# Four rewritten stages and an early half product in a two-block fp32 kernel

## The chip, the cores and the metric

One Trainium2 core of one chip. The time is the device time of one execution in microseconds (us), the median of a few runs; all data are fp32. Engines are TensorE (PE), VectorE (DVE), ScalarE (ACT), GpSimd (POOL) and SyncE (SP), which only starts transfers here.

## The reference

A sequence of 256 tokens of width 1024 goes through a first block of two hybrid attention layers and a second block. Cut to what the change touches:

```python
# first block, each of 2 layers
shift, scale, gate = split(c @ w_ada + b_ada)
h = split_cols((x * (1 + scale) + shift) @ w_in)          # three attention mixers on h
x = layer_norm(ALPHA * x + (1 + gate) * ((mix * silu(h["gate"])) @ w_out), ln_g, ln_b)
# second block
a_in = rms_norm(h_lat) * (1 + sc1) + sh1                  # and the same for a context
o = gdn_two_dirs(...)                                     # 4 chunks of 64 tokens, one after the other
y_a = u * (einsum(ws, rms_norm(v)) + bs)                  # chunk mixer, columns 0:512
y_b = rms_norm(o) * gdn_norm_g * silu(z)                  # from the recurrence, columns 512:1024
h_lat = h_lat + gt1 * (concat(y_a, y_b) @ w_out)
f_in = rms_norm(h_lat, norm2_g) * (1 + sc2) + sh2
aff = softmax(f_in @ w_router + b_router)                 # 16 experts
gate, idx = top_k(aff.T, 32)                              # each expert takes 32 tokens
ye = (silu(xe @ w_gate) * (xe @ w_up)) @ w_down * gate    # xe = f_in[idx]
h_lat = h_lat + gt2 * scatter_add(idx, ye)
return rms_norm(h_lat, final_norm_g)
```

## The kernel before, in words

Each engine has its own written-out program; semaphores order them. `tick`, `fill` and `drain` count events, `wait_ge(*at(event))` waits for one, `free(b)` waits until PSUM bank `b` (eight of 128x512) has been read. Tokens lie in two tiles `t` of 128.

**Weights.** All weights come as units of 2 MB in a fixed order (`unit_order`) that SP starts one by one, in order, each when its slot is free again (L495 to L502). There are 4 slots in `ring`; the experts (16, with 6 units each) use three more, which lie over `QKT`, `Vt_to_O` and `zuv_to_Kt`: the first is filled after the last `QS_mm`, the other two after `mix2` of tile 1. The first 7 expert units are thus in place before the experts begin; the eighth waits for the first expert product (`gu_mm` of expert 0).

**A layer's end.** `pe_y` multiplies the mixed rows by `w_out` in parts; `v_ln` gates, adds, takes the statistics (`bn_stats`, `bn_aggr`), waits for ACT's root (Ln, then Exp with scale -0.5) and normalizes, tile 0 then tile 1. Then the next layer begins: `pe_xT` transposes tile 0, `v_uT` and `a_uT` write its modulated rows, `pe_in` multiplies. DVE reaches `v_uT` of tile 0 only after `v_ln` of tile 1.

**The second block.** `pe_streams` begins after `a_ctx_T`; `a_lat_rs` and `v_lat_rows` normalize the rows; `pe_recur` steps through four chunks (products WS, QS, KV, AV). After it come the chunk mixer's product (`ws_mm`), `v_mix2` (norm of `O` and both halves of `wide`), and in `pe_mix2`, for each tile, two halves of four transposes and two column groups of eight products (128x512). `v_mix2` multiplies by `grow` (gt1), adds to `resid`; `a_route` takes the squares' sum and the root; `v_n2` scales rows; `pe_route` transposes them, `v_route` and `a_route` apply norm2_g, scale and shift into `fT`, and 16 router products (128x16) follow. Then softmax, four rounds of `max` and `match_replace`, a mask `selT`, its transpose, three products for positions, `Pone`, and the gather products `xe_mm` (16 of 128x512). POOL copies a column into `selg` so that `pe_grow(1)` can spread gt2 over rows; this and `v_grow(1)` stand ahead of the router.

**Experts and end.** Per expert: four `gu` units, activation, transposes, two `down` units, both halves of `ye` copied out of PSUM (ACT the first, DVE the second), and four products that accumulate in banks 0 to 3 (`moe_mm`). `v_final` multiplies by `grow`, adds `resid`, waits for ACT's squares and root, scales by it and by `fin_row`; SP sends out one tile at a time.

A fp32 product of 128x512 is two TensorE instructions in the trace, a transpose of 128x128 one.

## Time and profile before

| | us |
|---|---|
| median of 3 runs (lowest, highest) | 1344.79 (1342.96, 1347.21) |
| the profiled execution, device time | 1344.98 |
| its span on the core | 1343.2 |
| between the two | 1.8 |
| busy: PE, DVE, ACT, POOL | 1082.7, 429.4, 265.3, 70.0 |

The span is what the profiler sees of the core's engines; the device time has 1.8 us more. Busy shares say little here, since the kernel runs through stages with different limits; the rows below are read stage by stage.

### The profile page before, as it was taken

How to read it: one execution, taken by the hardware profiler on the slowest of the kernel's cores; microseconds unless marked ns; L12 is line 12 of the kernel's file. 1: busy time of each engine (PE TensorE's matmuls, PEld its weight loads, DVE VectorE, ACT ScalarE, POOL GpSimd, SP SyncE). 2: the span in 40 equal slices, each digit the busy share in tenths (PEclk: the TensorE clock that was granted, in tenths of full speed). 3: DMA queues.
4: the chain of work that ended last, by engine and by line, in shares of the span. 5: the costliest groups of instructions: out<-in, count | busy, mean ns of one | idle time of the engine just before them, and what ended most of it. 6: DMA issues, size and time to landing. Idle time of an engine off the chain costs nothing.

```text
span 1343.2 us, 17768 instructions
## 1 busy us (share of the span) xinstructions
PE 1082.7 (81%) x7516; PEld 585.2 (44%) x7516; DVE 429.4 (32%) x1023; ACT 265.3 (20%) x604; POOL 70.0 (5%) x81
## 2 busy tenths in 40 slices
PE   2899999889999999999988868687766666666663
PEld 0344774434576458975678844422221111121111
DVE  0135746323765445343256662400000000000003
ACT  0102134111213435442121343100000000000003
POOL 1001000000100000002204400000000000000000
PEclk9899989989989999899988889697798888889887
DMA  9773238523346961122110035079999999999993
GB/s 375 293 281 108 94 135 340 175 113 126 125 157 258 427 230 73 63 88 102 65 64 3 2 119 210 16 310 428 430 431 430 429 429 429 430 428 431 429 430 132
DMA packets 24270, 323.66 MB, mean 241 GB/s; under 512 B 2704, under 2 KB 2704, under 8 KB 4864
## 3 DMA queue, kind: packets, MB, share of 16 engines
q1 hardware_dynamic: 22160, 314.18, 57.1%
q0 software_dynamic: 2032, 8.35, 1.9%
q8 instruction: 60, 0.98, 0.3%
q14 instruction: 18, 0.15, 0.0%
HBM read 321.47 MB, written 1.05 MB: 240 GB/s over the span
## 4 chain that ended last, share of the span: by engine, by line
PE 54%; DMA 29%; DVE 9%; issue 4%; ACT 3%; POOL 0%; SPq 0%; DVEq 0%; ACTq 0%; POOLq 0%
PE banks L611 45%; DMA ring<-in_stream 18%; DMA Vt_to_O<-in_stream 7%; PE banks L622 2%; DMA zuv_to_Kt<-in_stream 2%; DMA QKT<-in_stream 2%; PE banks L2005 1%; PE banks L836 1%; PE banks L822 1%; DVE Vt_to_O L2263 1%; PE banks L857 1%; PE banks L819 1%; DVE probs L1169 1%; PE banks L723 1%; DMA grow<-in_rows 0%
## 5 line engine op out<-in xcount | busy, mean ns | idle before, releaser
L611 PE MATMUL banks<-ring,uT 128*128 128x512 f32 (+1 forms) x512 | 227.7, 600 | 13.7 <-DVE uT L1028 11.1
L611 PEld LDWEIGHTS banks<-ring,uT 128*128 128x128 f32 x512 | 97.3, 194 | 129.0 <-issue 123.3
L611 PE MATMUL banks<-ring,scr 128*32 128x512 f32 (+1 forms) x656 | 114.8, 695 | 48.0 <-DMA ring<-in_stream 46.0
L611 PE MATMUL banks<-ring,UWK 128*32 128x512 f32 (+1 forms) x368 | 85.9, 718 | 17.8 <-DMA ring<-in_stream 12.1
L2444 DVE SCALAR_TENSOR_TENSOR UWK<-UWK,banks 128x256 f32<-128x256 f32 x16 | 6.7, 421 | 292.5 <-ACT UWK L2697 292.5
L611 PE MATMUL banks<-scr 64*64 64x64 f32 (+2 forms) x2048 | 82.4, 234 | 6.5 <-DVE scr L2311 5.2
L611 PEld LDWEIGHTS banks<-ring,scr 128*32 128x32 f32 (+1 forms) x656 | 30.4, 127 | 125.3 <-DMA ring<-in_stream 70.2
L611 PEld LDWEIGHTS banks<-scr 64*64 64x64 f32 (+1 forms) x2048 | 79.2, 144 | 12.3 <-issue 5.6
L611 PE MATMUL banks<-UWK,ring 128*128 128x256 f32 x320 | 72.6, 386 | 2.1 <-DVE QKT L2087 1.7
L622 PE MATMUL banks<-ring,KC 128*32 128x512 f32 x384 | 50.7, 655 | 26.9 <-DMA ring<-in_stream 26.9
L2005 PE MATMUL banks<-UWK 128*128 128x512 f32 x128 | 58.7, 601 | 16.4 <-DVE UWK L2450 16.4
L611 PEld LDWEIGHTS banks<-UWK,ring 128*128 128x128 f32 x320 | 61.4, 193 | 12.5 <-DVE QKT L2087 2.5
L2697 ACT ACTIVATE UWK<-banks 128x256 f32<-128x256 f32 x16 | 6.1, 383 | 288.9 <-PE banks L611 288.9
L611 PE MATMUL banks<-uT,ring 128*128 128x256 f32 x256 | 60.1, 396 | 0.0
L611 PEld LDWEIGHTS banks<-ring,UWK 128*32 128x32 f32 (+1 forms) x368 | 28.2, 143 | 66.9 <-issue 46.0
L611 PEld LDWEIGHTS banks<-uT,ring 128*128 128x128 f32 x256 | 50.7, 201 | 7.4
L2450 DVE COPY UWK<-banks 128x512 f32<-128x512 f32 x16 | 11.1, 692 | 126.9 <-PE banks L611 126.9
L2005 PEld LDWEIGHTS banks<-UWK 128*128 128x128 f32 x128 | 23.0, 189 | 54.2 <-ACT UWK L2707 31.2
L1515 ACT ACTIVATE probs<-banks,mx 128x128 f32<-128x128 f32 x88 | 36.6, 418 | 45.6 <-DVE mx L1296 41.7
L611 PE MATMUL banks<-QKT,UWK 64*128 64x128 f32 (+2 forms) x192 | 35.5, 560 | 8.2 <-DVE QKT L2429 3.3
L535 POOL TENSOR_TENSOR scr<-scr,const 128x512 f32<-128x512 f32 x24 | 31.4, 1324 | 192.9 <-DVE scr L2218 130.4
L1050 DVE COPY H<-banks 128x512 f32<-128x512 f32 (+1 forms) x12 | 8.2, 681 | 93.7 <-PE banks L611 93.7
(365 smaller groups left out, 1246.8 us busy)
## 6 DMA issues: line engine op xcount, KB each, us to landing
ring<-in_stream SPq DMA_DIRECT2D x106, 2048.0 KB, 18.2
QKT<-in_stream SPq DMA_DIRECT2D x14, 2048.0 KB, 30.3
Vt_to_O<-in_stream SPq DMA_DIRECT2D x14, 2048.0 KB, 30.7
zuv_to_Kt<-in_stream SPq DMA_DIRECT2D x14, 2048.0 KB, 30.4
w<-in_w POOLq DMA_DIRECT2D x2, 1024.0 KB, 9.6
probs<-in_rows POOLq DMA_DIRECT2D x4, 512.0 KB, 5.1
const<-in_consts SPq DMA_DIRECT2D x1, 1215.0 KB, 5.9
resid<-in_x SPq DMA_DIRECT2D x1, 1024.0 KB, 24.1
```

What stands on the lines that cost most here:

```text
L535: pool.tensor_tensor(four(scr[:, t, M_, :], "all"), four(scr[:, t, AT_, :], "all"), four(const[:, lo:lo + 2 * CH], "dir"), ALU.mult).then_ ...
L611: return pe.matmul(o, a, b, start=start, stop=stop)
L622: ins = pe.matmul(bank[b][32 * j:32 * j + 32, :], window[:, j * (DCH // 4) + k, lo:lo + 32], w[:, j * (DCH // 4) + k, :], start=(n, k) == ...
L723: ins = pe.transpose(bank[b][0:rows, (2 * m + t) * P:(2 * m + t + 1) * P], f(t), ident)
L819: pe.matmul(bank[b + s][:, 0:P], q[:, 0:P], k[:, 0:P], start=True, stop=False)
L822: pe.matmul(bank[b + s][:, P:384], q[:, P:SEQ], k[:, :], start=False, stop=False)
L836: ins = pe.transpose(bank[4 + s][:, i * P:(i + 1) * P], probs[:, m % 3, s, i * P:(i + 1) * P], ident)
L857: pe.matmul(bank[6][HD * s:HD * s + HD, 0:SEQ], H[:, 0, v:v + HD], probT[:, m % 2, s, 0:SEQ], start=first and kind != "slc", stop=False)
L1169: dve.scalar_tensor_tensor(o, i, w, o, ALU.mult, ALU.add))
L1515: ins = act.activation(probs[:, i, s, lo:hi], bank[b + s][:, lo:hi], ACT.Exp, bias=mx[:, i, s, t:t + 1], accum_out=den[:, i, s, t:t + 1])
L2005: ins = pe.matmul(bank[2 * t + h][:, :], PgT[:, t, :], ye[:, h, 0:512], start=e == 0, stop=e == EXPERTS - 1)
L2263: ins = dve.scalar_tensor_tensor(state[:, i, :], state[:, i, :], egl[:, p // CH, TILES * s + t, i:i + 1], bank[b][:, h * P:(h + 1) * P], A ...
```

## The change

In the words of its author: "the four changes to end, router, layer 2 and roots, and the chunk mixer's half of the second block's output taken into the last step". What it does:

- *Roots*: every Ln and Exp pair for an inverse root becomes one Sqrt on ACT and a `reciprocal` on DVE (`inverse`).
- *Layer 2*: `pe_xT(l + 1, 0)` stands inside the last `pe_y` of layer 0, and `v_uT`, `a_uT` of tile 0 before the norm of tile 1.
- *Chunk mixer*: `pe_ws` and `v_mix_a` move into the last recurrence step, and `pe_mix2` multiplies the first four column blocks of both tiles before the last four.
- *Router*: the raw `resid` is transposed; norm2_g and scale go into the router's weights (`v_router`), the shift's part into a constant (`pe_const_logits`, `const_z`), the root is applied to the 16 logits. `n2` is made on ACT later. Positions come from a scan along the tokens, so the three position products and the mask multiplication go. `pe_grow(1)` moves behind `place_mm`, `v_grow(1)` into expert 0. POOL's copies `selb`, `selg` go: TensorE reads one column, broadcast.
- *End*: `resid` is put into banks 0 to 3 by identity products ahead of expert 0; gt2 multiplies `ye` on DVE (both halves); at the end ACT squares PSUM directly and DVE writes each half row block with one instruction, sent out by itself.

```diff
                 pe_ctx_T(pe)
             pe_y(pe, l, 1, 0, w_out, range(5, DCH))
-            pe_y(pe, l, 1, 1, w_out, range(0, DCH))
+            pe_y(pe, l, 1, 1, w_out, range(0, 5))
+            if l + 1 < DEPTH:
+                pe_xT(pe, l + 1, 0)
+            pe_y(pe, l, 1, 1, w_out, range(5, DCH))
...
+        def inverse(dve, ap, *event):
+
+            dve.reciprocal(ap, ap).then_inc(*tick("vector_step", *event))
+            dve.wait_ge(*last("vector_step"))
...
                 dve.wait_ge(*at("ln_rs", l, t))
+                inverse(dve, small_rs[:, t:t + 1])
                 r = resid[:, t, :]
                 dve.tensor_scalar(r, r, small_mv[:, t, 0:1], small_rs[:, t:t + 1], ALU.subtract, ALU.mult).then_inc(*tick("vector_step", "x_new", l + 1, t))
                 dve.wait_ge(*last("vector_step"))
                 if l == 0:
                     if t == 0:
-                        dve.wait_ge(*at("lngb", l))
+                        v_uT(dve, l + 1, 0)
                     continue
...
             if l == DEPTH - 1:
-                inv_root(act, rs2[:, 0:TILES], ssq[:, 0:TILES], D, "rs_ctx")
+                root(act, rs2[:, 0:TILES], ssq[:, 0:TILES], D, "rs_ctx")
             else:
-                act.activation(small_rs, C("ones")[:, 0:TILES], ACT.Ln).then_inc(*tick("scalar_step"))
+                act.activation(small_rs, C("ones")[:, 0:TILES], ACT.Sqrt).then_inc(*tick("scalar_step"))
...
-                act.activation(rs, small_mv[:, t, 1:2], ACT.Ln, bias=C("eps")[:, 0:1]).then_inc(*tick("scalar_step"))
-                act.wait_ge(*last("scalar_step"))
-                act.activation(rs, rs, ACT.Exp, scale=-0.5).then_inc(*tick("scalar_step", "ln_rs", l, t))
-                act.wait_ge(*last("scalar_step"))
-                if l == DEPTH - 1 and t == 0:
-                    a_ctx_T(act)
+                act.activation(rs, small_mv[:, t, 1:2], ACT.Sqrt, bias=C("eps")[:, 0:1]).then_inc(*tick("scalar_step", "ln_rs", l, t))
+                if t == 0:
+                    if l == DEPTH - 1:
+                        a_ctx_T(act)
+                    else:
+                        a_uT(act, l + 1, 0)
...
+            for h, b in enumerate(((3, 5), (5, 7))[i]):
                 pe.wait_ge(*free(b))
-                mm(pe, bank[b][:, :], selg[i][:, h, :], modrows[:, :], True, True).then_inc(*fill(b, "grow_mm", i, h))
+                mm(pe, bank[b][:, :], row_of(8 + 12 * i + 2 * h), modrows[:, :], True, True).then_inc(*fill(b, "grow_mm", i, h))
...
                 if n < 3:
                     pe_both_KV(pe, 1, n, (4, 5), new_v)
+                else:
+                    pe_ws(pe)
...
+            pe_const_logits(pe)
...
+        def pe_y2(pe, w, t, cg, half):
+            b = 4 + cg * 2 + t
+            if half == 0:
+                pe.wait_ge(*free(b))
+            if cg == 0:
+                pe.wait_ge(*at("m2T", t, half))
+            for k in range(4 * half, 4 * half + 4):
+                ins = mm(pe, bank[b], m2T[:, k, t * P:(t + 1) * P], w[cg][:, k, :], k == 0, k == DCH - 1)
+            if half:
+                ins.then_inc(*fill(b, "y2_mm", cg, t))
...
             w = [take(pe), take(pe)]
             for t in range(TILES):
...
+                pe_m2T(pe, t, 0)
+            pe_y2(pe, w, 0, 0, 0)
+            pe_y2(pe, w, 0, 1, 0)
+            pe_y2(pe, w, 1, 0, 0)
+            pe_m2T(pe, 0, 1)
+            pe_y2(pe, w, 1, 1, 0)
+            pe_m2T(pe, 1, 1)
+            pe_y2(pe, w, 0, 0, 1)
+            pe_y2(pe, w, 0, 1, 1)
+            pe_y2(pe, w, 1, 0, 1)
+            for half in range(2):
+                pe_route_T(pe, 0, half)
+            pe_y2(pe, w, 1, 1, 1)
+
+        def pe_route_T(pe, t, half):
+            b = 2 * t + half
+            pe.wait_ge(*at("h_lat", t, half))
+            pe.wait_ge(*free(b))
+            for m in range(4):
+                c = (4 * half + m) * P
+                ins = pe.transpose(bank[b][:, m * P:(m + 1) * P], resid[:, t, c:c + P], ident)
...
+        def pe_const_logits(pe):
+
+            pe.wait_ge(*at("router"))
+            pe.wait_ge(*free(3))
+            for k in range(DCH):
+                ins = mm(pe, bank[3][:, 0:EXPERTS], C("ones"), wab[:, k, :], k == 0, k == DCH - 1)
+            ins.then_inc(*fill(3, "const_mm"))
...
+            for half in range(2):
+                pe_route_T(pe, 1, half)
             pe.wait_ge(*free(4))
             for t in range(TILES):
-                pe.wait_ge(*at("fT", t, 0))
-                pe.wait_ge(*at("fT", t, 1))
                 for k in range(DCH):
+                    if k % 4 == 0:
+                        pe.wait_ge(*at("fT", t, k // 4))
...
+            pe.wait_ge(*at("place"))
             pe.wait_ge(*free(4))
             for t in range(TILES):
                 ins = pe.transpose(bank[4][:, t * EXPERTS:(t + 1) * EXPERTS], selT[0:EXPERTS, t * P:(t + 1) * P],
                                    ident[0:EXPERTS, 0:EXPERTS])
-            ins.then_inc(*fill(4, "sel_mm"))
...
+            ins.then_inc(*fill(4, "place_mm"))
+            pe_grow(pe, 1)
+            pe.wait_ge(*at("n2", 0))
+            pe.wait_ge(*at("n2", 1))
             pe.wait_ge(*at("Pone"))
...
+            for t in range(TILES):
+                for h in range(2):
+                    pe.matmul(bank[2 * t + h], ident, resid[:, t, h * 512:(h + 1) * 512], start=True, stop=False)
...
                     for h in range(2):
-                        ins = pe.matmul(bank[2 * t + h][:, :], PgT[:, t, :], ye[:, h, 0:512], start=e == 0,
+                        ins = pe.matmul(bank[2 * t + h], PgT[:, t, :], ye[:, h, 0:512], start=False,
                                         stop=e == EXPERTS - 1)
-                ins.then_inc(*fill(3, "moe_mm", e))
+                    if e == EXPERTS - 1:
+                        ins.then_inc(*tick("moe_done", "moe_mm", e, t))
...
+        def v_router(dve):
+
+            w = PR("router").rearrange("p (k e) -> p k e", e=EXPERTS)
+            dve.wait_ge(*at("ab_mm"))
+            dve.tensor_tensor(wab, w, over(mod[:, 24:32, 0], EXPERTS), ALU.mult).then_inc(*tick("vector_step"))
+            dve.wait_ge(*last("vector_step"))
+            dve.tensor_tensor(w, w, over(A2, EXPERTS), ALU.mult).then_inc(*tick("vector_step", "router"))
...
+                else:
+                    for t in range(TILES):
+                        v_mix_a(dve, t)
...
+            dve.wait_ge(*at("const_mm"))
+            dve.tensor_tensor(const_z, bank[3][:, 0:EXPERTS], RW("br"), ALU.add).then_inc(*drain(3, "const_z"))
+            for t in range(TILES):
                 dve.wait_ge(*at("rsh", t))
+                inverse(dve, rsh[:, 4 * t:4 * t + 4])
...
+                    dve.tensor_tensor(resid[:, t, c], resid[:, t, c], wide[:, t, c], ALU.add).then_inc(*tick("vector_step", "h_lat", t, cg))
+                    if t and cg == 0:
+                        v_fT(dve, 0)
+            v_fT(dve, 1)
...
+        def v_fT(dve, t):
+            b = 2 * t
+            dve.wait_ge(*at("fT_mm", t, 0))
+            dve.tensor_copy(fT[:, 0:4, t * P:(t + 1) * P], bank[b].rearrange("p (m s) -> p m s", m=4)).then_inc(*drain(b, "fT", t, 0))
...
+            dve.wait_ge(*at("rs_h"))
+            inverse(dve, rs2[:, 0:TILES], "rs_row")
+            for t in range(TILES):
+                ins = dve.scalar_tensor_tensor(aff[:, t, :], bank[4][:, t * EXPERTS:(t + 1) * EXPERTS], rs2[:, t:t + 1],
+                                               const_z, ALU.mult, ALU.add)
...
+            chosen, count = selT[0:EXPERTS, :], affT[0:EXPERTS, :]
+            dve.tensor_scalar(chosen, w, 10 * NEG, None, ALU.is_lt).then_inc(*tick("vector_step"))
+            dve.wait_ge(*last("vector_step"))
+            dve.tensor_tensor_scan(count, C("ones")[0:EXPERTS, 0:1].broadcast_to([EXPERTS, SEQ]), chosen, 0.0,
+                                   ALU.mult, ALU.add).then_inc(*tick("vector_step"))
+            dve.wait_ge(*last("vector_step"))
+            dve.tensor_tensor(chosen, chosen, count, ALU.mult).then_inc(*tick("vector_step", "place"))
+            dve.wait_ge(*at("place_mm"))
+            for t in range(TILES):
+                ins = dve.tensor_tensor(Pone[:, t, :, :], times(C("iota"), EXPERTS),
+                                        over(bank[4][:, t * EXPERTS:(t + 1) * EXPERTS], CAP), ALU.is_equal)
...
+                if e == 0:
+                    v_grow(dve, 1)
+                dve.wait_ge(*at("down0_mm", e))
+                dve.tensor_tensor(ye[:, 0, 0:512], bank[4], grow[:, 0:512], ALU.mult).then_inc(*drain(4, "ye", e, 0))
                 dve.wait_ge(*at("down_mm", e, 1))
-                dve.tensor_copy(ye[:, 1, 0:512], bank[5][:, :]).then_inc(*drain(5, "ye", e, 1))
-                dve.wait_ge(*drained(5))
+                dve.tensor_tensor(ye[:, 1, 0:512], bank[5], grow[:, 512:D], ALU.mult).then_inc(*drain(5, "ye", e, 1))
...
-            dve.wait_ge(*at("moe_mm", EXPERTS - 1))
-            for t in range(TILES):
+            dve.wait_ge(*at("fin_row"))
+            for t in range(TILES):
+                dve.wait_ge(*at("rs_out", t))
+                inverse(dve, rs2[:, t:t + 1])
...
-                    b = 2 * t + h
                     c = slice(h * 512, (h + 1) * 512)
...
+                    dve.scalar_tensor_tensor(resid[:, t, c], banks[t][:, h, :], rs2[:, t:t + 1], fin_row[:, c], ALU.mult,
+                                             ALU.mult).then_inc(*tick("vector_step", "result", t, h))
...
+        def root(act, o, i, n, *event):
+
+            act.activation(o, i, ACT.Sqrt, bias=C("eps")[:, 1:2], scale=1.0 / n).then_inc(*tick("scalar_step", *event))
...
+            for t in range(TILES):
+                copy(t, 0)
...
+            root(act, rs2[:, 0:TILES], ssq[:, 0:TILES], D, "rs_h")
+            act.activation(lowest, C("ones")[:, 0:1], ACT.Exp).then_inc(*tick("scalar_step"))
+            act.wait_ge(*at("rs_row"))
+            for t in range(TILES):
+                act.activation(n2[:, t, :], resid[:, t, :], ACT.Copy, scale=rs2[:, t:t + 1]).then_inc(*tick("scalar_step", "n2", t))
...
-                act.wait_ge(*at("down0_mm", e))
-                act.activation(ye[:, 0, 0:512], bank[4][:, :], ACT.Copy).then_inc(*drain(4, "ye", e, 0))
-                act.wait_ge(*drained(4))
...
+            act.activation(lowest, C("ones")[:, 0:1], ACT.Sqrt).then_inc(*tick("scalar_step"))
+            for t in range(TILES):
+                act.wait_ge(*at("moe_mm", EXPERTS - 1, t))
+                act.activation(uwk[:, 512:512 + D].rearrange("p (a n) -> p a n", a=2), banks[t][:, :, :], ACT.Square,
+                               accum_out=ssq[:, t:t + 1]).then_inc(*tick("scalar_step"))
...
+                root(act, rs2[:, t:t + 1], ssq[:, t:t + 1], D, "rs_out", t)
```

## Rows read from the trace of the kernel before

**Rows 1.** The page: the span, and the chain that ended last by engine.

```profile
span 1343.2 us, 17768 instructions
...
PE 54%; DMA 29%; DVE 9%; issue 4%; ACT 3%; POOL 0%; SPq 0%; DVEq 0%; ACTq 0%; POOLq 0%
```

**Rows 2.** Busy time by stage; columns are us, then busy (count) by engine, clock, DMA share, GB/s.

```profile
792.00:796.00 4.00, 0.00 (x0) 0.00 (x0) 3.90 (x9) 2.98 (x4) 0.00 (x0) 0.66 0.46 197
...
836.00:880.00 44.00, 28.66 (x102) 17.76 (x104) 18.01 (x43) 6.51 (x14) 0.53 (x1) 0.71 0.09 33
842.00:850.00 8.00, 6.98 (x32) 6.90 (x32) 2.12 (x8) 0.02 (x1) 0.43 (x1) 0.50 0.00 0
881.00:1319.00 438.00, 296.89 (x1911) 85.29 (x1900) 23.84 (x47) 27.35 (x63) 0.00 (x0) 0.86 1.00 427
```

**Rows 3.** Timeline (start us, us busy) where the first layer ends.

```profile
249.87 14.86 PE L611 MATMUL banks<-ring,uT 128*128 128x512 f32 x34
...
272.96 9.54 PE L611 MATMUL banks<-ring,uT 128*128 128x512 f32 x16 [7.36 <-DVE uT L1028]
...
285.24 4.96 PE L611 MATMUL banks<-ring,uT 128*128 128x512 f32 x11 [1.86 <-DVE uT L1028]
```

**Rows 4.** Timeline where the second layer ends and the second block begins.

```profile
502.40 10.60 PE L611 MATMUL banks<-UWK,ring 128*128 128x256 f32 x48 [0.45 <-ACT UWK L2490]
...
513.77 3.72 PE L611 MATMUL banks<-UWK,ring 128*128 128x256 f32 x16 [0.78 <-DVE QKT L2087]
...
518.37 10.63 PE L611 MATMUL banks<-UWK,ring 128*128 128x256 f32 x48 [0.88 <-DVE QKT L2087]
```

**Rows 5.** Timeline of the last recurrence step and the output product.

```profile
788.80 2.05 PE L611 MATMUL banks<-zuv_to_Kt,par 128*128 128x128 f32 x16
...
798.69 16.36 PE L611 MATMUL banks<-ring,scr 128*128 128x512 f32 x32 [0.24 <-ACT scr L2660]
...
814.89 1.04 PE L1904 MATMUL banks<-const,wide 128*128 128x128 f32 x8
...
816.27 13.97 PE L611 MATMUL banks<-ring,scr 128*128 128x512 f32 x32 [0.34 <-ACT scr L2660]
```

**Rows 6.** Timeline of TensorE from the router to the first expert.

```profile
842.29 6.98 PE L611 MATMUL banks<-par,UWK 128*128 128x16 f32 x32 [3.96 <-DVE UWK L2385]
...
850.98 0.59 PE L1936 MATMUL banks<-const,lows 128*16 128x128 f32 x2 [1.71 <-DVE lows L2406]
...
856.29 0.39 PE L1941 MATMUL banks<-const,UWK 16*128 16x16 f32 x2 [4.72 <-DVE UWK L2417]
...
861.76 15.57 PE L611 MATMUL banks<-QKT,UWK 128*128 128x512 f32 x32 [3.26 <-DVE QKT L2429]
...
878.67 3.64 PE L611 MATMUL banks<-ring,scr 128*32 128x512 f32 x32 [1.35 <-DVE scr L2435]
```

**Rows 7.** Busy time inside 64 narrow TensorE instructions (128x16), 534.0 to 544.8 us.

```profile
534.00:536.00 2.00, 2.00 (x21) 2.00 (x19) 1.81 (x5) 1.24 (x5) 0.00 (x0) 1.00 0.00 0
...
542.00:544.00 2.00, 2.00 (x11) 2.00 (x11) 0.00 (x0) 0.00 (x0) 0.00 (x0) 0.50 0.00 0
```

**Rows 8.** Timeline of the end.

```profile
1319.91 1.95 PE L611 MATMUL banks<-zuv_to_Kt,UWK 128*32 128x512 f32 x16 [1.13 <-DMA zuv_to_Kt<-in_stream]
...
1322.89 3.67 PE L2005 MATMUL banks<-UWK 128*128 128x512 f32 x8 [1.03 <-DVE UWK L2450]
...
1338.90 1.23 DVE L2468 TENSOR_TENSOR resid<-resid,UWK 128x1024 f32<-128x1024 f32 x1
```

**Rows 9.** Groups of one shape: count, busy us, mean ns of one.

```profile
L1372 DVE SCALAR_TENSOR_TENSOR resid<-resid,wide 128x512 f32<-128x512 f32 x8 | 5.5, 692 | 0.3
...
L1303 DVE RECIPROCAL rin<-den 128x4 f32<-128x4 f32 x22 | 3.7, 168 | 0.0
...
L1559 ACT ACT_TABLE_LOAD x3 | 3.8, 1283 | 18.2 <-DVE small L1376 18.2
...
L2713 ACT ACTIVATE UWK<-resid 128x1024 f32<-128x1024 f32 x2 | 2.1, 1057 | 6.9 <-DVE resid L2461 6.8
```

241 lines of the change are left out of this document (82 added, 159 removed).

## The prediction

> **What bounds the kernel now.** I read the page first, for the span and its ending chain, then busy time by stage, then the timeline at each seam that the change touches, and last the groups by shape for prices. The span is 1343.2 us, and TensorE holds 54% of the chain that ended last, transfers 29% [rows 1]. That is an average over two regimes, which the stages tell apart [rows 2]. From 881 to 1319 us, the experts, the transfers are busy all the time (1.00, 427 GB/s) while TensorE is busy 296.9 of 438 us: this stage lasts as long as its bytes, counted from the moment the first expert product frees a slot. Ahead of it, from 836 to 880 us, the transfers are nearly idle (0.09), because all seven slots are full and nothing has been consumed. So each microsecond taken out of TensorE's way to the first expert product moves the whole saturated stage forward, although that stage can't be made shorter. The same holds for every seam further up, as the weights are requested when earlier ones are used. What comes after the last unit (1319.91 [rows 8]) is latency in full.
>
> The reader is to see four seams. At the end of the first layer TensorE waits 7.36 us for DVE, then runs 9.54 us on 16 instructions that take 7 us elsewhere, and waits 1.86 us for tile 1 [rows 3]. At the start of the second block it waits 0.45, 0.78 and 0.88 us [rows 4]. After the recurrence it does nothing for four microseconds and its granted clock falls (0.66 in that stretch [rows 2]), so the first output product takes 16.36 us where the second takes 13.97 [rows 5]. And from the output product's end (816.27 + 13.97 = 830.24) to the first expert product at 878.67 lie 48.4 us of short steps [rows 5, 6].
>
> **Prices.** A product of 128x512 costs 13.97 / 16 = 0.87 us at full clock, eight transposes 1.04 [rows 5]. A DVE instruction over 512 columns takes 0.69, the reciprocal 0.17, ACT's squares over 1024 columns 1.06, a table load 1.28 [rows 9]; small DVE and ACT instructions I take at 0.2 to 0.3, near the reciprocal.
>
> **First layer's end.** The last `pe_y` runs 17 products from 249.87 for 14.86 us [rows 3]. With tile 0's transposes inside it, after 14 of them (262.1), they end at 263.1; tile 0's norm is then ready: its sums can begin at 254.3, take six DVE instructions (4.3), root, reciprocal and scaling 1.6, so 260.2. From transposes to the next product 1.86 us pass for tile 1 [rows 3], so tile 0 would be ready at 264.9, and TensorE comes free at 249.87 + 14.86 + 1.04 = 265.8: no wait, and no fall of the clock. The product takes 7.0, tile 1's transposes 1.04, the 1.86 us stay: 275.7 in place of 285.24. I take -9.7, since part of these 0.87 overlap. DVE now works at tile 0's rows before tile 1's norm; tile 1's is ready near 270.3, needed at 272.8, so it has 2.5 us to spare. The layer's own Exp needs a table load again, on an idle ACT.
>
> **Second block's start.** Here ACT and DVE carry two table loads less per root, some 2.6 us, on both tiles. The three waits are 0.45, 0.78 and 0.88 us, each shorter than that: -2.1. The first Tanh pays one load, 1.28 us, behind which TensorE has 24 products queued that don't need it. `v_router` is two small DVE instructions in a stretch where DVE idles; uncovered it would be 0.4 us.
>
> **Output product.** `pe_ws` takes the attention product's place, one microsecond before 788.80, and lasts 2.05 [rows 5]: 789.8. The attention product behind it costs 1.1 (that microsecond): 790.9. What waits for it, DVE's sums and squares of `O`, is some 2.4 us later than before, as DVE also does `v_mix_a` first; these feed only the second half, which starts some 10 us later. The constant logits are 16 narrow instructions: 21 of them took 2.00 us at full clock, 11 at half [rows 7], so 1.5 or 2.9; I take 1.6, as TensorE has been busy. Transposes 1.04, ACT's copy some 0.3 beyond them: the products begin at 793.8. 32 products (27.9) and 16 transposes in between (2.1): 823.8 for 830.24, -6.4.
>
> **Router.** From the last product: DVE's two instructions and their waits 1.5, transposes 0.5, then 32 narrow instructions, 3.1 us at full clock by rows 7 and 6.98 in half clock as before [rows 6]. I take 4.2, since tile 0's half can begin at full clock: 6.3 in all, where it was 849.27 - 830.24 = 19.0. -12.7. What is gone is root, scaling, transposes and eight pieces of `fT` in a row, and `v_grow`'s wait for its transfer.
>
> Logits to `affT`: before 850.98 - 849.27 = 1.7 us [rows 6]. Now the reciprocal comes first, and ACT has two copies for `n2` (1.06 each) in its queue ahead of the softmax's Exp, because they start at the reciprocal, 0.7 us before the Exp's input is ready. That makes 3.5 us: +1.8.
>
> Top-k: one copy out of PSUM less, about -0.4. Then the scan and a multiplication over 16x256 are added ahead of the transpose. No scan is in the trace: from below 0.35 (half of the 512-column price), from above 0.69; I take 0.6, for a scan carries a value along. With the multiplication +1.0. Behind the transposes TensorE has `pe_grow`'s 4 instructions before the gather's 32; the two `is_equal` (1.4 us) hide under it. Before, transposes at 856.29 to the gather's end 877.33 took 21.0 us [rows 6]; now 1.0 + 0.4 + 36 instructions at 0.437 + 2.0 for clock (the 32 took 1.6 us more than 13.97) = 19.1: -1.9. Then four identity products stand ahead of the first expert product, priced as the four of `moe_mm`: +3.7 [rows 8]. Nothing covers them. The second `grow` now holds bank 7 until DVE has done expert 0's activation, some 2 us of TensorE; transfers have four units in queue then, so it is hidden; bare it would be 2.
>
> Sum for output to experts: -6.4 - 12.7 + 1.8 - 0.4 - 1.9 + 3.7 = -15.9.
>
> **Experts.** DVE does both halves of `ye`: +0.7 us per expert on TensorE's way, against 141 us of idle in 15 intervals, 9.4 each [rows 2]. Zero, except after the last unit: +0.5.
>
> **End.** Before: products end at 1326.56, DVE at 1340.13 [rows 8], 13.6 us. Now for tile 1: squares 1.06 and their sum 0.2, root 0.3, reciprocal 0.2, two half rows 1.4, hand-overs 0.4: 3.5. Tile 0 starts two products sooner and is out of the way. The last transfer carries half the bytes; between nothing and 0.3 us, I take nothing. -10.1 + 0.5 = -9.6.
>
> **Sum.** -9.7 - 2.1 - 15.9 - 9.6 = -37.3 from 1344.98, the profiled execution (1343.2 span and 1.8 around it): 1307.7. It stands 0.2 above the median of the runs, which I neglect.
>
> **Rivals.**
>
> *The clock falls at the constant logits.* In 64 narrow instructions the clock went from 1.00 to 0.50, that is from 2.4 to 1.2 GHz, with TensorE busy throughout (2.00 of 2.00 us [rows 7]). Sixteen are a quarter of that, but they stand just ahead of the output product. Price: 1.4 for themselves and 2.4 for the product (16.36 - 13.97 [rows 5]), and the router at half clock throughout 2.8: about 1314. Against it: the clock held over at least 21 of the 64. The Trainium skill, "TensorE: Matmul & The Clock Gate", Part 1, describes the low level as the idle one, which activity releases; by that rule alone the sum stands, and the trace doesn't agree with it in rows 7.
>
> *Squares and copies need tables of their own.* If Square, Copy or Identity can't run beside Sqrt, loads come back at each alternation, some six of them with 1.28 us on the way: 1307.7 + 8 = 1316. Against it: before, ACT's squares at the end ran with no load in front of them, 1.06 us for 1024 columns, and the loads of that kind stand at a root's line [rows 9]. The Trainium skill, "ScalarE: Activation LUTs", Table sets, says that cheap functions are in every set; by it this rival would be nothing, and the trace agrees so far, for Square beside the tables of Ln and Exp; beside Sqrt's it shows nothing.
>
> *The first layer's gain is given back* in the second layer's attention, where the modulation weights stream. If their transfers were not requested earlier, up to 9.7 us return: 1317. Against: SP starts each by a TensorE event.
>
> *Slower, by the experts becoming DVE's.* If the two multiplications held TensorE for longer than the 9.4 us of idle per expert, the stage would grow; to end above 1345 it needs 9.4 + 37.3 / 16 = 11.7 us per expert. The price by rows is 0.7, a seventeenth. The profile would show transfers below 1.00.
>
> **How the numbers follow.** Forecast as summed 0.72 (its own range 1303 to 1311, from the bounds: narrow instructions -1.1 to +2.8, constant logits +1.4, scan 0.25, clock at the gather 2, runs 2), clock 0.14, tables 0.05, gain given back 0.04, experts 0.02, no change to be seen 0.01, and 0.02 for something faster than 1301. The range 1301 to 1316 takes in the first two. Faster by over 0.3% (4 us, what a measurement of this kernel can tell from no change) 0.97, within 0.01, slower 0.02.
>
> **What would show it.** Tile 1's first product of layer 2 near 275.7, with no half-clock stretch before it; the first expert product near 851 (878.67 - 27.7); 438 us of saturated transfers after it, unchanged; 3.5 us from the last product to DVE's end. The sum is wrong if the expert stage changes its length, or if the clock stays low through the output product.

## The result and the profile after

The changed kernel takes 1303.35 us (median of 4 runs, 1301.45 to 1304.21) where the kernel before, run beside it, takes 1346.0 (4 runs, 1342.96 to 1349.5): a ratio of 0.9697, 95% interval 0.9661 to 0.9733. The forecast was 1307.7, with a range of 1301 to 1316. The profiled execution took 1302.77 us, its span 1301.0, so the span fell by 42.2 us where the sum said 37.3.

The page of the changed kernel, its span and its ending chain (compare [rows 1]):

```profile
span 1301.0 us, 17728 instructions
...
PE 58%; DMA 29%; DVE 7%; issue 3%; ACT 1%; another core or an unknown queue 1%; SPq 0%; POOL 0%; DVEq 0%; ACTq 0%; POOLq 0%
```

DVE went from 9% to 7% and ACT from 3% to 1% of the chain: less of the path is small work of these two. The timeline of TensorE at the first layer's end (compare [rows 3]):

```profile
249.53 12.29 PE L602 MATMUL banks<-ring,uT 128*128 128x512 f32 x28
261.65 1.04 PE L654 MATMUL banks<-const,resid 128*128 128x128 f32 x8
262.52 9.61 PE L602 MATMUL banks<-ring,uT 128*128 128x512 f32 x22
...
274.84 17.41 PE L602 MATMUL banks<-ring,uT 128*128 128x512 f32 x40 [1.84 <-DVE uT L1022]
```

Tile 0's transposes stand inside the last product of the first layer, the next layer's products follow in the same row of 22 with no wait, and only tile 1's 1.84 us are left. Where the second block begins (compare [rows 4]) the three waits are gone, and all 112 instructions up to the transposes are one row:

```profile
490.01 24.34 PE L602 MATMUL banks<-UWK,ring 128*128 128x256 f32 x112
...
519.39 8.76 PE L602 MATMUL banks<-small,UWK 128*128 128x16 f32 x64
```

From the last recurrence step to the first expert (compare [rows 5, 6]):

```profile
771.82 2.02 PE L602 MATMUL banks<-zuv_to_Kt,par 128*128 128x128 f32 x16 [0.63 <-issue]
773.77 1.09 PE L602 MATMUL banks<-QKT,Vt_to_O 64*64 64x128 f32 x16
774.79 1.96 PE L602 MATMUL banks<-small,const 128*128 128x16 f32 x16
...
778.01 10.54 PE L602 MATMUL banks<-ring,scr 128*128 128x512 f32 x24 [0.34 <-ACT scr L2709]
...
809.47 5.00 PE L602 MATMUL banks<-par,UWK 128*128 128x16 f32 x32
817.78 0.60 PE L1971 MATMUL banks<-const,lows 128*16 128x128 f32 x2 [3.32 <-DVE lows L2461]
823.82 0.39 PE L1976 MATMUL banks<-const,UWK 16*128 16x16 f32 x2 [5.44 <-DVE UWK L2482]
824.15 3.78 PE L602 MATMUL banks<-modrows,const 128*128 128x512 f32 x4
827.72 14.32 PE L602 MATMUL banks<-QKT,UWK 128*128 128x512 f32 x32
843.33 3.67 PE L1999 MATMUL banks<-resid,const 128*128 128x512 f32 x8 [1.28 <-DVE scr L2497]
846.93 3.64 PE L602 MATMUL banks<-ring,scr 128*32 128x512 f32 x32
```

The long stop behind the recurrence is gone. The 16 constant logits took 1.96 us, and the granted clock was 1.00 in them and in the output product behind them. The longest waits that remain here are 3.32 us, for the softmax, and 5.44 us, for the ranking. The experts in the windows (compare [rows 2]):

```profile
848.00:1286.00 438.00, 298.21 (x1917) 85.43 (x1912) 34.19 (x64) 19.88 (x50) 0.00 (x0) 0.86 1.00 426
```

The transfers are as saturated as before. From the first expert's first product to the last output products it is 444.8 us (846.93 to 1291.74), and 444.2 before. The end, all engines (compare [rows 8]):

```profile
1291.74 3.67 PE L2039 MATMUL banks<-UWK 128*128 128x512 f32 x8 [1.58 <-DVE UWK L2516]
1293.73 1.02 ACT L2764 ACTIVATE UWK<-banks 128x1024 f32<-128x1024 f32 x1 [7.77 <-PE banks L2039]
...
1295.45 1.02 ACT L2764 ACTIVATE UWK<-banks 128x1024 f32<-128x1024 f32 x1 [0.28 <-PE banks L2039]
...
1296.92 0.16 DVE L1358 RECIPROCAL small<-small 128x1 f32<-128x1 f32 x1
1297.12 1.41 DVE L2525 SCALAR_TENSOR_TENSOR resid<-banks,small,UWK 128x512 f32<-128x512 f32 x2
```

Tile 0's squares run while TensorE still multiplies, and the last product is followed by 3.1 us of work. The whole span, laid out by the stretches of the two traces (us; negative is shorter). The last step is counted up to its last attention product before (787.78) and up to `pe_ws`, which has that place, now (771.82):

| stretch | forecast | measured |
|---|---|---|
| up to layer 2's attention (356.06 to 345.86) | -9.7 | -10.2 |
| layer 2's narrow stretch, rest of layer 2 | 0 | -1.65, -0.5 |
| start of the second block, 502.40 to 534.03 and 490.01 to 519.39 | -2.1 | -2.25 |
| the 64 narrow instructions; from there to the last step | 0 | -2.0, +0.6 |
| last step to the output product's end (807.47) | -6.4 | -6.8 |
| router (ends 814.47) | -12.7 | -12.0 |
| logits to `affT` | +1.8 | +1.6 |
| top-k and scan, to the placement (823.82) | +0.6 | +0.7 |
| placement to the gather's end (842.04) | -2.9 | -2.8 |
| identity products | +3.7 | +3.55 |
| experts, to the last unit's output products | +0.5 | +0.6 |
| those to the end of the span | -10.1 | -11.05 |
| sum | -37.3 | -42.2 |

### The profile page after: what moved, and what is told of

It is laid out like the page before. It is cut to its first block, busy times and chain, and to the rows that moved or that the text cites. A ratio compares the mean times of both kernels' runs of the same rounds, so it can differ in the third digit from the quotient of the medians.

```text
span 1301.0 us, 17728 instructions
## 1 busy us (share of the span) xinstructions
PE 1073.4 (83%) x7534; PEld 576.8 (44%) x7534; DVE 430.2 (33%) x1039; ACT 225.9 (17%) x550; POOL 64.3 (5%) x73
## 4 chain that ended last, share of the span: by engine, by line
PE 58%; DMA 29%; DVE 7%; issue 3%; ACT 1%; another core or an unknown queue 1%; SPq 0%; POOL 0%; DVEq 0%; ACTq 0%; POOLq 0%
PE banks L602 48%; DMA Vt_to_O<-in_stream 14%; DMA ring<-in_stream 10%; PE banks L613 3%; DMA QKT<-in_stream 2%; DMA zuv_to_Kt<-in_stream 2%; PE banks L2039 1%; PE banks L826 1%; DVE Vt_to_O L2309 1%; PE banks L847 1%; PE banks L812 1%; PE banks L809 1%; PE banks L713 1%; DVE probs L1163 1%
## 5 line engine op out<-in xcount | busy, mean ns | idle before, releaser
L602 PE MATMUL banks<-ring,uT 128*128 128x512 f32 (+1 forms) x512 | 225.0, 595 | 6.3 <-DVE uT L1022 3.7
L602 PE MATMUL banks<-ring,scr 128*32 128x512 f32 (+1 forms) x656 | 112.8, 696 | 38.8 <-DMA ring<-in_stream 38.5
L602 PE MATMUL banks<-ring,UWK 128*32 128x512 f32 (+1 forms) x368 | 91.4, 786 | 15.1 <-DMA ring<-in_stream 10.5
L2514 DVE TENSOR_TENSOR UWK<-banks,grow 128x512 f32<-128x512 f32 x16 | 11.1, 692 | 127.0 <-PE banks L602 118.1
```

Source lines behind the costliest of these rows:

```text
L602: return pe.matmul(o, a, b, start=start, stop=stop)
```

## The experiments

All are edits of the changed kernel. A median of four runs is a blunt measure here: the changed kernel again has 1305.15 where it had 1303.35, and its single runs go from 1301.61 to 1309.17. The stretches of the traces repeat much better: from the router's first product to the first expert's, 37.46 us in both traces of the changed kernel. So the readings go by stretches, and the medians stand beside them. "Again" is the second trace of the changed kernel.

| kernel | median us | span in its trace | ratio to before, 95% |
|---|---|---|---|
| after_again | 1305.15 | 1299.8 | 0.9719 (0.9683 to 0.9755) |
| layer2_undone | 1310.68 | 1308.4 | 0.9762 (0.9727 to 0.9796) |
| mixer_late | 1307.51 | 1305.1 | 0.9737 (0.9703 to 0.9770) |
| ln_exp_roots | 1312.89 | 1310.6 | 0.9775 (0.9745 to 0.9804) |
| seed_late | 1301.31 | 1295.5 | 0.9683 (0.9629 to 0.9738) |
| grow_early | 1302.22 | 1300.4 | 0.9686 (0.9635 to 0.9737) |
| exp_first | 1300.92 | 1296.7 | 0.9656 (0.9623 to 0.9689) |
| all_three | 1299.39 | 1296.3 | 0.9655 (0.9618 to 0.9692) |
| end_undone | 1307.33 | 1306.7 | 0.9721 (0.9690 to 0.9752) |
| narrow_x4 | 1314.23 | 1314.7 | 0.9798 (0.9724 to 0.9871) |
| two | 1296.69 | 1295.3 | 0.9646 (0.9616 to 0.9677) |
| warm | 1298.93 | 1303.9 | 0.9670 (0.9630 to 0.9709) |

**The same kernel again.** No edit.

> The changed kernel once more, with nothing altered: 1303 us, within 2 us. It is here for two stretches of its trace. In the profile of after the 64 products of the gate's a and b took 8.76 us against 10.72 before, and the stretch of narrow products in layer 2 was 1.6 us shorter than before; nothing in the change shortens either. If their length is a matter of when the clock falls and so varies from one execution to the next, at least one of the two differs here from the execution of after by 0.5 us or more; if the change itself brought it, both come out as in the profile of after (ab 8.8 us) within 0.2 us.

The 64 narrow instructions kept their length (8.45 us for 8.76). Layer 2's narrow stretch did not: from the attention's rotation to the products with `PC` 54.87 us for 56.54, 1.7 less in the same kernel. Over all traces it has two lengths with the new roots, 54.9 (six times) and 56.5 (six times), and 58.2 in the two kernels with the old roots. The windows of before, after and again over it say what differs (TensorE's busy time is the second number, the granted clock the third from the right):

```profile
356.06:414.25 58.19, 57.89 (x316) 46.05 (x315) 36.55 (x117) 11.42 (x30) 0.79 (x1) 0.94 0.34 124
```

```profile
345.86:402.40 56.54, 56.25 (x316) 44.76 (x315) 36.54 (x117) 11.43 (x30) 0.79 (x1) 0.97 0.34 127
```

```profile
346.19:401.06 54.87, 54.57 (x316) 43.64 (x314) 36.55 (x117) 11.45 (x30) 0.79 (x1) 1.00 0.35 131
```

TensorE is idle for 0.3 us in each of the three, and DVE's and ACT's work is the same: the three lengths differ by the granted clock alone.

The 64 instructions, start to next start, take 8.2 to 8.8 us in eleven traces, and 11.2 in two, end_undone and warm, whose code there is that of after. Before's is 10.6. The mean granted clock over them is 0.65 before, 0.81 in after, and 0.61 in end_undone. Two rows of warm's windows inside the 64, to stand beside [rows 7]:

```profile
520.00:522.00 2.00, 2.00 (x20) 2.00 (x19) 1.82 (x6) 1.32 (x4) 0.00 (x0) 1.00 0.02 4
522.00:524.00 2.00, 2.00 (x13) 2.00 (x13) 1.93 (x7) 1.93 (x6) 0.00 (x0) 0.57 0.00 0
```

The clock falls within them in all fourteen traces; how much of them is left at the half clock is what varies. Before's 10.6 us lie inside the spread of one and the same code, 8.2 to 11.2, so the 2.0 us "gained" there can't be credited to the change.

**Layer 2's order undone.**

```
-            pe_y(pe, l, 1, 1, w_out, range(0, 5))
-            if l + 1 < DEPTH:
-                pe_xT(pe, l + 1, 0)
-            pe_y(pe, l, 1, 1, w_out, range(5, DCH))
+            pe_y(pe, l, 1, 1, w_out, range(0, DCH))
```

with `v_uT` and `a_uT` of tile 0 back in the second layer's own loops.

> Of the change only the layer 2 part is undone: tile 0 of the second layer is normalized and transposed after all of the first layer's output product. The theory of the prediction: a wait of 7.4 us and products at the half clock worth 2.7 us come back, less the wait of 1.8 us that after has there and the few products that after does beforehand; 1303 + 10 = 1313 us. The first product of layer 2's tile 1 runs again at some 285 us. Rival, that a good part of the gain came from a clock that went on falling earlier or later elsewhere: then the narrow stretch of layer 2 gets longer as well and the total is 1315 us or above; rival, that the wait is filled otherwise: 1306 us or below.

```profile
251.51 14.86 PE L602 MATMUL banks<-ring,uT 128*128 128x512 f32 x34
...
271.94 9.20 PE L602 MATMUL banks<-ring,uT 128*128 128x512 f32 x16 [4.70 <-DVE uT L1018]
...
283.88 8.39 PE L602 MATMUL banks<-ring,uT 128*128 128x512 f32 x19 [1.87 <-DVE uT L1018]
```

This is the timeline of [rows 3] again, with one difference: tile 0's wait is 4.70 us, not 7.36. From the last product's start to tile 1's product it is 32.4 us here, 25.3 in after, 35.4 before. So undoing the order costs 7.1 us where the expectation had 10, and the form of the root, which stays new here, is worth the other 3.0 of the 10.1 us at this place. The rest of the span's 8.6 us stood ahead of this place (251.51 for 249.85).

**The mixer's half late.** `pe_ws` back behind the last step's attention product, `v_mix_a` and ACT's first copy behind the step, `pe_m2T` and `pe_y2` tile by tile.

```
             pe_m2T(pe, 0, 0)
             pe_m2T(pe, 0, 1)
             pe_y2(pe, w, 0, 0, 0)
             pe_y2(pe, w, 0, 0, 1)
```

> Of the change only the order around the last recurrence step is undone: the chunk mixer's half of the second block's output product is multiplied after the last step again, and its products stand behind those of each tile as before. The prediction made this part worth 6.4 us (measured 6.8): TensorE idles for DVE and ACT behind the last step and y2 starts at a fallen clock. Expected 1309.5 us (1308.5 to 1311), and a granted clock below 1.00 in the first 4 us of the output product. Rival, that the other part of the change at this place (one root instead of the exponential form) already took the waits away and the order is worth little: 1305 us or below.

```profile
771.31 2.05 PE L602 MATMUL banks<-zuv_to_Kt,par 128*128 128x128 f32 x16
...
778.74 1.09 PE L1907 MATMUL banks<-const,wide 128*128 128x128 f32 x4 [3.68 <-DVE wide L2388]
```

A wait of 3.68 us is back. Before it was longer, with the old roots:

```profile
796.04 1.09 PE L1904 MATMUL banks<-const,wide 128*128 128x128 f32 x4 [5.19 <-DVE wide L2351]
```

The first windows of mixer_late's output product say what the wait costs beyond itself:

```profile
778.00:780.00 2.00, 1.09 (x4) 0.72 (x4) 1.90 (x6) 0.13 (x1) 0.00 (x0) 0.50 0.00 0
780.00:784.00 4.00, 3.92 (x10) 2.23 (x11) 2.62 (x8) 1.06 (x2) 0.00 (x0) 0.68 0.33 61
```

From `pe_ws` to the router's first product 42.4 us for 37.7, and `pe_ws` itself one attention product (1.0) later: 5.8 us, near the 6.4 expected, though the median, 1307.51, lies below the 1308.5 to 1311 that were given. The span shows 5.3 against again, with 2.0 less ahead of layer 2's attention and 1.7 more in the stretch behind it.

**The roots by logarithm and exponential again.**

```
-            act.activation(o, i, ACT.Sqrt, ...)
+            act.activation(o, i, ACT.Ln, ...)
+            act.activation(o, o, ACT.Exp, scale=-0.5)
```

and no reciprocal on DVE.

> Of the change only the form of the roots is undone: every square root with its reciprocal on DVE is a logarithm and an exponential on ACT again, everywhere. Between the two stands a table load of 1.28 us each, and another before the next. Price by the places where a root ends last: the start of the second block 2.9 us, the end of the last recurrence step and the router's row of roots 1 to 2 us each, the final norm 2.5 to 5 us; together 7 to 10 us if all of them are on the path, so 1310 to 1313 us. Rival, that the new order has made these roots late nowhere but at the final norm and the start of the second block: 1307 to 1308.5 us. Rival, that the form of the root costs nothing anywhere since ACT has time: 1303 to 1304.5 us.

The span is 10.8 us above again's, and this is where: 0.8 at the first layer's end, 3.4 in layer 2's narrow stretch (58.24 for 54.87; 1.7 against after's; the mean granted clock there is 0.94), 0.7 in the rest of layer 2, 2.3 at the start of the second block (31.66 us for 29.37; before's was 31.63), nothing between the last step and the router (37.66 for 37.65), nothing to the first expert (37.2 for 37.5), 3.9 at the end. The last is read in the timeline of ACT and DVE:

```profile
1303.57 1.28 ACT L2532 ACT_TABLE_LOAD   x1
1304.87 0.29 ACT L2532 ACTIVATE small<-small,const 128x1 f32<-128x1 f32 x1
1305.18 1.28 ACT L2534 ACT_TABLE_LOAD   x1
...
1306.71 1.41 DVE L2527 SCALAR_TENSOR_TENSOR resid<-banks,small,UWK 128x512 f32<-128x512 f32 x2 [2.78 <-ACT small L2534]
```

Two loads in one root of 3.1 us, where after's root and reciprocal took 0.5. The first tile's root has a load too, and the second tile's squares wait behind it on ACT. The form of the root thus explains the whole gain at the second block's start, and nothing of it between recurrence and experts, where the new order covers it.

**Identity products in the first expert's wait.** They move behind the first group of gate and up products of expert 0.

```
                     ins.then_inc(*fill(6, "gu_mm", e, i))
+                if e == 0:
+                    for t in range(TILES):
+                        for h in range(2):
+                            pe.matmul(bank[2 * t + h], ident, resid[:, t, h * 512:(h + 1) * 512], start=True, stop=False)
```

> The four products with the identity, which put the stream into the output banks, move from ahead of the first expert's first product to behind the first group of its gate and up products, where TensorE idles 3 us for the gathered rows. Theory of the prediction (the 3.7 us stand on the path where they are): 1303 - 3.6 = 1299.5 us (1299 to 1300.5). Rival, that the experts run on at the pace of the weights' transfers (DMA share 1.00 from 848 us) and the start of the first expert doesn't set their end: 1303 us, with the last expert ending at 1288 us as before.

```profile
841.64 3.64 PE L602 MATMUL banks<-ring,scr 128*32 128x512 f32 x32 [1.35 <-DVE scr L2498]
...
848.64 3.70 PE L2011 MATMUL banks<-resid,const 128*128 128x512 f32 x8
852.27 0.64 PE L2015 MATMUL banks<-const,QKT 128*32 128x128 f32 x16
```

Router to first expert 33.92 us for 37.46, and the last output products still start 444.7 us after the first expert's first product (444.8 in after): all 3.5 us arrive at the end. After's wait of 2.99 us for `grow` in front of line 2014 is gone too. That the experts' time is counted from their first product is shown here directly. The median, 1301.31, is above the 1299 to 1300.5 expected, with single runs from 1297.35 to 1309.89; the reading rests on the stretches.

**The growth products early.** `pe_grow(pe, 1)`, into banks 6 and 7, right behind the affinities' transposes, and DVE's sum behind `Pg`.

```
             ins.then_inc(*fill(5, "affT_mm"))
+            pe_grow(pe, 1)
...
             ins.then_inc(*fill(4, "place_mm"))
-            pe_grow(pe, 1)
```

> The growth of the ranking counts for the first expert's rows (four products at the half clock, 3.8 us) moves from behind the placement, where the gather's products wait for it, to ahead of it, where TensorE waits for the scan. If TensorE there only waits and the products fill the wait: 2.0 to 3.5 us less, 1300 us. Rival, that DVE's copy of its result, which now stands ahead of the gather's last copy, delays the gather by 1 to 1.4 us: 1301 to 1302.5 us. By the rival of transfers that set the experts' pace nothing changes: 1303 us.

```profile
822.14 0.29 PE L1977 MATMUL banks<-const,UWK 16*128 16x16 f32 x2 [2.03 <-DVE UWK L2482]
824.13 17.02 PE L602 MATMUL banks<-QKT,UWK 128*128 128x512 f32 x32 [1.70 <-DVE QKT L2485]
```

The gather starts 2.0 us after the placement in place of 3.9, as meant, and takes 17.02 us in place of 14.32. Router to first expert 38.26 for 37.46: 0.8 lost, where 2.0 to 3.5 less were expected. Two windows of this kernel, and again's for 828 to 830 us behind them, tell why (TensorE's instructions in 2 us, and the granted clock in the third column from the right):

```profile
826.00:828.00 2.00, 2.00 (x4) 0.97 (x3) 0.54 (x1) 0.01 (x1) 0.00 (x0) 0.50 0.00 0
828.00:830.00 2.00, 2.00 (x3) 0.69 (x3) 0.00 (x0) 0.77 (x1) 0.00 (x0) 0.50 0.00 0
```

```profile
828.00:830.00 2.00, 2.00 (x6) 0.84 (x5) 0.00 (x0) 0.78 (x1) 0.00 (x0) 1.00 0.00 0
```

Where after has the growth products, TensorE runs them at the half clock while it waits for DVE's comparison anyway, and the gather behind them is at the full clock after its first products. TensorE is busy throughout the gather in both, so DVE's sum, the rival, doesn't hold it; the mean granted clock over the gather is 0.82 here and 0.97 in after. Neither theory had this.

**The exponential first.** ACT takes the softmax's Exp ahead of `n2`.

```
+            act.activation(aff, aff, ACT.Exp)
             for t in range(TILES):
                 act.activation(n2[:, t, :], resid[:, t, :], ACT.Copy, scale=rs2[:, t:t + 1])
-            act.activation(aff, aff, ACT.Exp)
```

> ACT does the exponential of the router's softmax ahead of the copies of the normed rows (2.2 us of them stood before it in the profile of after). If the softmax's chain is what the affinities' transposes wait for: 1.3 to 2.1 us less, 1301.5 us. Rival, that the copies are then late for the rows' products and give it back: 1303 us.

Router to `affT` 7.38 us for 8.3: 0.9 less, not 1.3 to 2.1, since its input is ready only 6.3 us after the router's first product, when ACT in after is half through the copies (5.2 to 7.4 us). Of it 0.3 to 0.4 go in a longer gather (14.69 for 14.32): 0.6 net. The span is 3.1 us below again's all the same: 3.1 are gained between the modulation's row products and the last step (208.6 us for 211.8), where the two kernels are the same, and 0.6 are lost ahead of layer 2's attention. That is luck.

**The three together.**

> The three of this call in one kernel: the identity products in the first expert's wait, the growth of the counts ahead of the placement, the exponential ahead of the copies. Independent, they add up: 3.6 + 2.5 + 1.5 = 7.6 us less, 1295.5 us (1294.5 to 1297.5). If the weights' transfers set the experts' end: no less than 1302 us. If they share a wait (the earlier gather has the weights of the first expert still on their way): 1298 to 1300 us, with a wait of TensorE for a DMA at the first expert.

Router to first expert 32.54 us: 4.9 less than after, where 7.6 was expected, with no wait for a transfer. The parts are 3.5 and 0.6 from the runs above, and 0.8 left for the early growth, which alone had lost that much.

**The two without the growth.**

> The identity products in the first expert's wait and the exponential ahead of the copies, with the growth of the counts left where after has it. By the traces of the last call the first is worth 4.1 us, the second 0.9 us and the early growth nothing, since the gather behind it ran longer at the half clock: 5 us less than after, span 1295 to 1296.5 us. If the early growth did bring something within the three: the span is 1 us or more above that of the three together (1296.3 us, of which 1.3 us stood ahead of the router).

33.36 us, span 1295.3, median 1296.69. So within the three the early growth did bring 0.8 us, though alone it cost as much: there the gather took 15.87 us at a mean granted clock of 0.88, alone 17.02 at 0.82, and here, without it, 14.66 at 0.95. By these traces its sign hangs on the clock; each kernel has one trace, so how often it comes out either way is not shown. The spans (1296.3 and 1295.3) differ by what stood ahead of the router. This is the best median of the study, 6.7 us below after's. The two ratio intervals just overlap; the 4.1 us of stretches don't depend on them.

**Useless products for the clock.** all_three with four identity products into bank 0, one ahead of `affT`, two behind the growth, one behind the placement.

```
+        def warm(pe, n):
+            for _ in range(n):
+                pe.matmul(bank[0], ident, resid[:, 0, 0:512], start=True, stop=True)
```

> The three together, and four products of no use beside them (identity times a part of the stream into bank 0, which the gather overwrites): one ahead of the affinities' transposes, two behind the growth, one behind the placement, all in TensorE's waits. If the gather lost its 2.3 us of earlier start to the clock, as the windows of the early growth show (0.50 to 830 us, against 826.6 us with the growth behind the placement): the clock is back at 1.00 by the gather's first products, the gather takes 14 us or less instead of 15.9, and the first expert's first product comes 1.5 to 2.5 us earlier after the router than in the three. Rival, that the gather is held by something else, such as DVE's sum for the growth in front of its copies: no shorter. Rival, that the useless products end late themselves: up to 1 us lost.

```profile
830.00:832.00 2.00, 1.13 (x4) 0.49 (x4) 1.54 (x4) 0.00 (x0) 0.00 (x0) 1.00 0.00 0
832.00:834.00 2.00, 1.35 (x3) 0.65 (x3) 1.97 (x4) 0.00 (x0) 0.00 (x0) 0.73 0.00 0
834.00:838.00 4.00, 4.00 (x8) 1.56 (x7) 1.22 (x2) 0.78 (x1) 0.00 (x0) 0.71 0.00 0
```

The clock did come back to 1.00 ahead of the gather, and then fell again in its first part, behind a stretch with TensorE busy 1.13 of 2 us. The gather took 15.67 us for 15.87, router to first expert 32.46 for 32.54: nothing, where 1.5 to 2.5 us were expected. In the traces of these kernels the gather's length goes with its mean granted clock (14.32 us at 0.97, 14.66 at 0.95, 15.87 at 0.88, 17.02 at 0.82); a filling that keeps the clock up was not found.

**The end undone.** ACT copies half of `ye`, `moe_mm` alone in the banks, the stream added on DVE, squares from the stream, one transfer for each tile; the root keeps its new form.

> Of the change only the end is undone: no identity products ahead of the first expert, ACT copies half of each expert's output as before, the stream is added on DVE at the end, squares from the stream, one output transfer for each tile. The form of the roots stays that of after. By the trace of after the new end is worth 10.45 us to the last DVE instruction and 0.6 us behind it, of which the identity products give back 3.55: net 7.5 us. Part of the 10.45 belongs to the form of the last root (one table load of 1.28 us and an exponential less, 1.6 to 2.5 us), which stays here. Expected: 5 to 6 us slower than after, span 1305 to 1306 us, the first expert's first product 3.6 us earlier. Rival, that the experts' pace is set by the weights' transfers and so the earlier start gives nothing: 8.5 to 9.5 us slower, span 1308.5 to 1309.5 us.

From the last output products to the end of the span 16.7 us for 9.3: 7.5 more; router to first expert 33.94 for 37.46: 3.5 less. Net 3.9, below the 5 to 6 expected, because the last root's form is worth 3.9 (ln_exp_roots) and not 1.6 to 2.5: 7.5 + 3.9 = 11.4, near the 11.05 that both together brought. The span is 6.9 above again's, since 2.9 more stand at the 64 narrow instructions.

**The constant logits four times over.** Only repeated work is added.

```
+            for _ in range(4):
                 for k in range(DCH):
```

> The 16 narrow products (128x16) between the last recurrence step and the output product are done four times over, 64 in a row with nothing else, and only the repetition is added. They were 16 products in 1.96 us at a granted clock of 1.00 in after, and the 64 of a and b fell to 0.50 after some 5 us. If the clock holds: 5.9 us more. If it falls within the row as it did at a and b: a row of 64 of about 8.4 to 8.8 us (6.5 to 6.8 us more) and an output product that begins at the half clock, another 1 to 3 us; together 7.5 to 10 us, span 1307 to 1310 us. Rival, that the fall at a and b comes from something else than the narrow products (the transposes or the wait ahead of them): the clock stays at 1.00 through all 64.

```profile
777.81 11.72 PE L602 MATMUL banks<-small,const 128*128 128x16 f32 x64
```

```profile
778.00:780.00 2.00, 2.00 (x20) 2.00 (x19) 1.77 (x5) 0.00 (x0) 0.00 (x0) 1.00 1.11 475
780.00:782.00 2.00, 2.00 (x12) 2.00 (x12) 1.93 (x3) 0.00 (x0) 0.00 (x0) 0.54 0.41 172
```

The clock fell between 780 and 782 us and stayed at 0.50 to its end, with TensorE busy throughout; last step to router 49.1 us for 37.7, 11.5 more, above the 7.5 to 10 expected. The rival, that the fall at the 64 of a and b comes from the transposes or the wait ahead of them, is out: at a second place, with other work ahead, a row of 64 brings it too, and a row of 16 there does not. Sixteen of them took 1.86 to 1.96 us in the other traces.

## Why the prediction held, and where it was off

- First layer's end: forecast -9.7 (its own figures, 285.24 and 275.7, give 9.5), measured -10.2, product of tile 1 at 274.84. The prediction priced order and root together, and that was right. What each is worth depends on which is undone first: without the new order 7.1 us are lost and the root's form has 3.0; with the new order kept, the old root costs 0.8.
- Second block's start: -2.1 against -2.25, all of it the form of the root (31.66 us with the old form, 29.37 with the new). The rest of layer 2, taken at nothing, has a small part of it too: 88.2 us in the two kernels with the old roots, 87.4 to 87.7 in the twelve with the new.
- Output product: -6.4 against -6.8; undone by itself 5.8. The steps named are in the rows: no long wait (0.34 us), no half clock, and the constant logits, taken at 1.6 us, at 1.96.
- Router: -12.7 against -12.0. The 32 narrow instructions took 5.00 us, the term was 4.2, which had more of them at the full clock. This is the largest term, and no run undoes it by itself: that the new arithmetic brings it is read from the two traces, and ln_exp_roots shows only that the root's form has no part in it.
- Logits to `affT` +1.8 (+1.6), scan and multiplication +1.0 (0.68 and 0.41 us in the trace), placement to the gather's end -2.9 (-2.8), identity products +3.7 (+3.55). "Nothing covers them" was true of the identity products where they stand, and seed_late showed where a cover is, 10 us later: TensorE's wait of 2.99 us for the second `grow`, ahead of 856.99.
- Experts +0.5 (+0.6), transfers at 1.00 throughout.
- End: -10.1 against -11.05. The larger part of the difference is the last transfer, taken at nothing: 2.5 us from DVE's last instruction to the end of the span for 3.1. The rest is the work behind the last product, 3.1 us for the 3.5 summed.

The 4.9 us between sum and span are, then: 2.0 at the 64 narrow instructions and 1.65 in layer 2's narrow stretch, both a matter of the granted clock in that execution; 0.95 at the end; 0.5 in the rest of layer 2; 0.5 at the first seam; less 0.7 over all else. The first is luck, since the same code varies there by 3.0 us, and the second may be, since the same kernel varies there by 1.7. Without the two the span would have fallen by 38.5 us, 1.3 more than the sum. Whether the old root makes the clock fall more often in layer 2's stretch stays open: both kernels with it took 58.2 us and none of the twelve with the new root more than 56.6, but TensorE waits no longer there, and two traces are few.

Of the rivals, the clock at the constant logits did not fall (1.00, 1.96 us), though narrow_x4 shows that its mechanism is real, and begins within 64 of them. No table was loaded for Square, Copy or Identity beside Sqrt: at the end ACT goes from squares to root to squares to root with no load (1293.73 to 1296.59), from Copy to roots to Copy at 777.27 to 789.02, and from Identity to root to Identity at 262.78 to 273.10. The first layer's gain was not given back: the 7.1 us of layer2_undone arrived at its end, with 1.7 from ahead of that place a span 8.6 longer. The experts did not become DVE's: the transfers stayed at 1.00, and end_undone, where ACT does half of `ye` again, needs 444.7 us for the experts too.

## What to carry to other kernels

A stage that lasts as long as its bytes doesn't hide what stands ahead of it, if its transfers wait for its first consumer: here what was taken from the way there arrived at the end, 3.5 of 3.5 us for the identity products. So look for work ahead of such a stage that can stand in a wait inside it. And before moving a matrix product into an earlier wait, look at the clock behind its old place: the growth products took 3.8 us where they stood, and moving them alone into an idle stretch started the gather 2.0 us sooner and lost 0.8 in all, since the gather ran 2.7 us longer.

## What the hardware showed that was not expected

- The granted clock of the same code differs from one execution to the next: the 64 narrow instructions took 8.2 to 8.8 us in eleven traces and 11.2 in two, and from the modulation's row products to the last step it was 208.6 to 215.8 us over traces whose code there is alike (exp_first and warm).
- In rows of 64 narrow instructions, at two places of the program, TensorE fell from 2.4 to 1.2 GHz though it was busy all the time: 20 of them in 2 us at 1.00, then 11 in 2 us at 0.50. In rows of 16 it did not fall.
- A logarithm followed by an exponential costs a table load of 1.28 us ahead of each, 3.1 us for a root of one column; a square root with DVE's reciprocal took 0.5 with no load beside squares and copies.
- The scan over 16x256 took 0.68 us, the multiplication of the same shape 0.41; the prediction had 1.0 for the two.
